# HGRN2 stage on one Trainium2 core: where ScalarE makes the high part of a head's second dense unit

## What is computed

```python
def hgrn2_mixer(h, w_in, lb, gn_g, w_out):
    z = h @ w_in
    q, f_raw, i, g = jnp.split(z, 4, axis=-1)
    f = lb + (1.0 - lb) * jax.nn.sigmoid(f_raw)
    log_f = jnp.log(f)
    k = 1.0 - f
    ...
    # per head and chunk; bt is the running sum of log_f
        decay = jnp.exp(jnp.where(tril[:, :, None], diff, -jnp.inf))
        scores = jnp.einsum('bhtk,bhsk,bhtsk->bhts', qt, kt, decay)
        o = (jnp.einsum('bhts,bhsv->bhtv', scores, vt)
             + jnp.einsum('bhtk,bhkv->bhtv', qt * jnp.exp(bt), S))
    ...
    o = o * lax.rsqrt(jnp.mean(o * o, axis=-1, keepdims=True) + EPS)
    o = o * gn_g.reshape(HG_HEADS, HG_DV)
    o = o.reshape(B, T, D_HG) * jax.nn.silu(g)
    return o @ w_out
```

## Time and profile before

| | |
|---|---|
| median of 3 runs | 1831.57 us (1830.7 to 1832.07) |
| the profiled execution | 1832.15 us, its span 1830.4 us |
| busy: TensorE, VectorE, ScalarE, GpSimd | 1784.8, 837.5, 647.2, 719.2 us |
| granted TensorE clock, mean | 0.994 of full speed |
| HGRN2 stage (eight heads) | about 1155 to 1422 us from the span's start |

### The profile page before, as it was taken

The page is one execution under the profiler, slowest core; times in us unless marked ns, Lnnn a source line. Parts: engine busy times, 40 slices in busy tenths (PEclk is TensorE's granted clock), DMA queues, the critical chain, the costliest instruction groups (busy, mean ns, idle before and its releaser), DMA issues.

```text
span 1830.4 us, 23909 instructions
## 1 busy us (share of the span) xinstructions
PE 1784.8 (98%) x8198; PEld 1444.1 (79%) x8198; DVE 837.5 (46%) x1472; ACT 647.2 (35%) x930; POOL 719.2 (39%) x315
## 2 busy tenths in 40 slices
PE   8999999999999999999999999999999999999998
PEld 7788778888888784788888888777777788888886
DVE  4644565333333698533242335456565432322425
ACT  5545343222222431532222224454544432222222
POOL 3222225444444375344444353332322344344441
PEclk9999999999999999999999999999999999999999
DMA  8331123322232131233223233221221233232221
GB/s 217 90 96 50 56 71 104 102 94 92 92 102 93 58 98 36 77 96 114 93 84 107 84 103 92 70 81 57 70 67 46 78 113 97 80 115 92 91 93 46
DMA packets 149749, 160.00 MB, mean 87 GB/s; under 512 B 10147, under 2 KB 110999, under 8 KB 149695
## 3 DMA queue, kind: packets, MB, share of 16 engines
q1 hardware_dynamic: 148879, 158.50, 28.2%
q10 hardware_dynamic: 816, 0.79, 0.1%
HBM read 156.63 MB, written 2.62 MB: 87 GB/s over the span
## 4 chain that ended last, share of the span: by engine, by line
PE 52%; issue 30%; POOL 10%; DVE 6%; ACT 1%; POOLq 0%; DVEq 0%; ACTq 0%
PE ps L1095 46%; POOL wlo L585 9%; DVE ps L2000 2%; PE ps L1269 2%; PE ps L1403 2%; PE ps L1258 1%; DVE ss L1617 1%; DVE acc L1639 1%; DVE h_lo L1605 0%; PE ps L1233 0%; PE ps L1234 0%; POOL wlo L596 0%; DVE xT L1642 0%; DVE apad L1978 0%; DVE sq L1798 0%
## 5 line engine op out<-in xcount | busy, mean ns | idle before, releaser
L585 POOL TENSOR_TENSOR wlo<-raw,whi 128x1024 fp32r<-128x1024 f32 x272 | 654.8, 2422 | 1034.5 <-ACT whi L652 1020.3
L1095 PE MATMUL ps<-h_hi,wlo 128*128 128x512 f32 x1472 | 589.7, 401 | 6.4 <-POOL wlo L585 4.2
L1095 PE MATMUL ps<-h_hi,whi 128*128 128x512 f32 x1472 | 576.3, 391 | 0.0
L1095 PE MATMUL ps<-h_lo,whi 128*128 128x512 f32 x1472 | 575.6, 391 | 0.0
L652 ACT ACTIVATE whi<-raw 128x1024 fp32r<-128x1024 f32 x282 | 292.0, 1054 | 504.8 <-PE ps L1095 504.8
L1095 PEld LDWEIGHTS ps<-h_hi,wlo 128*128 128x128 f32 x1472 | 277.6, 189 | 66.7 <-POOL wlo L585 5.1
L1095 PEld LDWEIGHTS ps<-h_hi,whi 128*128 128x128 f32 x1472 | 277.2, 188 | 59.3
L1095 PEld LDWEIGHTS ps<-h_lo,whi 128*128 128x128 f32 x1472 | 277.6, 189 | 58.3 <-issue 3.1
L1095 PE MATMUL ps<-m_hi,wlo 128*128 128x512 f32 x800 | 320.6, 401 | 1.5 <-DVE m_lo L1818 1.4
L1095 PE MATMUL ps<-m_hi,whi 128*128 128x512 f32 x800 | 317.1, 396 | 0.0
L1095 PE MATMUL ps<-m_lo,whi 128*128 128x512 f32 x800 | 317.1, 396 | 0.0
(11 more groups left out here) (259 smaller groups left out, 1426.7 us busy)
## 6 DMA issues: line engine op xcount, KB each, us to landing
raw<-in_ffn_w SPq DMA_DIRECT2D x264, 256.0 KB, 2.9
raw<-in_w_ff SPq DMA_DIRECT2D x128, 256.0 KB, 2.9
raw<-in_hg_w_in SPq DMA_DIRECT2D x64, 256.0 KB, 3.2
raw<-in_w_in SPq DMA_DIRECT2D x40, 256.0 KB, 4.1
raw<-in_cp_w_in SPq DMA_DIRECT2D x24, 256.0 KB, 3.0
raw<-in_w_out SPq DMA_DIRECT2D x16, 256.0 KB, 2.9
raw<-in_cp_w_out SPq DMA_DIRECT2D x16, 256.0 KB, 3.0
raw<-in_hg_w_out SPq DMA_DIRECT2D x16, 256.0 KB, 2.9
```

Of the source, the lines that this page charges most:

```text
L585: pool.tensor_tensor(wlo[:, u % RING, :, :], raw[:, u % RING, :, :], whi[:, u % RING, :, :].bitcast(F32), ALU.subtract).then_inc(unit_lo, 1)
L1095: mm = pe.matmul(ps[:, b, :], wt[:, s, a, m * P:(m + 1) * P], xt[:, kts[a], :], start=starts and a == 0 and i == 0, stop=last)
```

## The change

In `core` on ScalarE, `units(1)` moves from behind `level_rows(0)` to the front, ahead of `head_norm` and `level_rows(0)`. In the last head's table of dense tiles on TensorE, one tile more is made behind level three (index 2: tiles 8 to 10 in place of 8 and 9), one less behind level six (index 5: tile 15 alone in place of 14 and 15); those between keep their number and move on by one.

```diff
+                units(1)
                 if before_it is not None:
                     head_norm(before_it)
                 level_rows(0)
-                units(1)
                 act.wait_ge(filled[5], nth("hg", "vt", n))
...
             core(HG_HEADS - 1, lambda lo, hi: pieces_of(lo, hi, hgout), HG_HEADS - 2,
-                 ((4, 6), (6, 8), (8, 10), (10, 12), (12, 14), (14, 16), (16, 17), (17, 18), (18, 20), (20, 24)))
+                 ((4, 6), (6, 8), (8, 11), (11, 13), (13, 15), (15, 16), (16, 17), (17, 18), (18, 20), (20, 24)))
```

## The result

The changed kernel takes **1818.2 us** in the median of four runs (1817.56 to 1823.12), the kernel before 1831.82 (four runs, 1830.7 to 1832.66): a ratio of 0.9932 with a 95% interval of 0.9914 to 0.995, about 13.6 us less. The forecast was 1818.4, with a range of 1815.8 to 1821.9. The median lies within it; one of the four runs, 1823.12 us, lies outside.

What follows compares the result with a forecast made beforehand. TensorE, busy 98% of 1830.4 us, was taken as the bound, with its waits for rows to win. Six steady heads at 1.9 plus 1.85 for the last gave 13.2 us off 1831.57: 1818.4 us, range 1815.8 to 1821.9.

Steps and rivals of the forecast that it cites:

- The bound and the cause: HGRN stage: TensorE waits for ScalarE's rows (15.7 us) because GpSimd's subtraction holds the first-level key product 1.85 us.
- (c): Rival: the 1.85 us belong to the first level's fine stride, the copy only changes place; 1831.6 us, chance 0.03.
- The cover of the copy: ScalarE, steady head: moved copy costs zero, with 0.9 us left before the norm and 0.7 us more behind level-one rows.
- Where the collision goes: Steady head: GpSimd waits and ends at 1265.3, or the spans' doubling waits and ends near 1265.0; neither costs anything.
- The margin before the key product: VectorE, steady head: 0.9 us left between the moved collision and the key product at 1266.24.
- A steady head: Six steady heads: each wins 1.9 us, as level two starts earlier on TensorE.
- the bound 1.85 of my own two: Steady head: gain if the VectorE and ScalarE chain holds all the way, 1.85 us instead of 1.9.
- The last head: Chain-bound, gains 1.85 us; the moved tile, bounded by 0.62 won and 0.70 lost, is taken as 0.
- The first head: Level one 0.7 to 0.9 us late, absorbed by TensorE's 2.83 us wait; clock gain between 0 and 1.3, taken as 0.
- its staying up: Rival: first head's TensorE clock stays up, 1.3 us more, 14.5 us in all or 1817.1 us; chance 0.13.
- The sum: Whole kernel: 6 x 1.9 + 1.85 = 13.25, rounded to 13.2 us; span 1817.2, median 1818.4 us.
- (d): Rival: in-order ScalarE stands at the moved wait, released late; at 1265.7 it is 7.0 us slower, 1838.6 us; chance 0.03.

Runs made afterwards that it cites:

- e3: Kernel before, ScalarE's order kept, with GpSimd's subtraction of the moved unit held until VectorE has grown all seven levels: 1814.72 us, ratio 0.9908.
- e4: Changed kernel, with GpSimd's subtraction of the moved unit held until ScalarE has copied the values (vh), about its old place: 1829.49 us, ratio 0.9983.
- e8: Changed kernel plus loads of another ScalarE table and back (2.56 us) between moved copy and norm, heads two to eight: 1824.73 us, ratio 0.9958.
- e2: Kernel before with the second hunk alone (last head's tile moved, copy at its old place): 1832.18 us, ratio 1.0001.
- e1: Changed kernel without its second hunk (copy moved, last head's tiles as before): 1818.35 us, ratio 0.9917.
- e7: Changed kernel with the same ScalarE table load written twice between moved copy and norm, heads two to eight; only one took place: 1817.14 us.
- e6: Changed kernel with one more ScalarE table load (1.28 us) between moved copy and norm, heads two to eight: 1822.77 us in its one execution.
- v1: Changed kernel with both first-head copies made earlier, the first ahead of the gates, the second ahead of the table load: 1814.13 us, ratio 0.9901.
- v2: e3 with the first head's first copy made ahead of the gates: 1813.91 us, ratio 0.9899.

## Why the prediction was right, and where it was not

- **The bound and the cause** held: the key product was held by GpSimd's subtraction, 1.85 us a head. Holding the subtraction away from the product (e3) and back upon it (e4) shows it from both sides, and the rival that the first level is slow by itself (c) is out: 0.426 us.
- **The cover of the copy** held: copy forecast at 1261.1 against a first dense matmul at 1260.64, measured 0.30 us of waiting behind the table's load, so 0.3 us after its end; 0.9 us of idle time left, measured 0.93. The total cover was put at 1.6 us and e8 says 1.4 to 1.5.
- **Where the collision goes** was given with two ends, and the second came: the doubling waits (2.61 us), and GpSimd is held by the query besides (2.62 instead of 2.38). The margin before the key product was put at 0.9 us and is 1.12. One reading was wrong: the trace of before does hold a subtraction that finds VectorE in such a product. The second one of the first head starts at 1166.50 us, 0.34 before the end of the key product, and takes 2.54 us, the first 2.40; the earlier trace rows show them as one line. So the rows of before already held what came after: GpSimd held up by a VectorE product. The two subtractions, shortest, median and longest in ns:

```profile
L585 POOL TENSOR_TENSOR wlo<-raw,whi x2: 2397/2470/2544, 1164.2 to 1166.5; 128x1024 fp32r<-128x1024 f32 x2
```

- **A steady head**: 1.9 us forecast; measured 1.82 in the head that was followed and 1.84 in the mean of six (11.04 us against 11.4, 0.4 too much). The mis-sized term is the 0.05 us by which I let TensorE and not the chain set level two. Level two of the changed kernel starts at 1262.52, after its operand, and still has the longer form of a product that waited (0.72 us, not 0.62), so the bound 1.85 of my own two was the nearer one; the gain at level two is 3.75 - 1.90 = 1.85.
- **The last head**: 1.85 forecast, 1.84 measured, and the tile at zero, with the wait before level seven where it was foretold (0.50 us; I had 0.7).
- **The first head** was the step that failed in the profiled execution. I took 0 for the clock and gave its staying up 13 in 100; it stayed up, 1.5 us. Level one was 0.6 us late (I had 0.7 to 0.9), and the idle time was not the same in all: 0.46 + 2.11 = 2.57 us, before 2.83. But no argument by the length of the gaps alone would do: the clock falls in some executions and not in others with the same two gaps (below). It was a toss-up that I treated as a constant.
- **The sum** for the profiled execution: 11.04 + 1.84 + 1.5 = 14.4, against 13.2. It began the stage 0.25 us later than the kernel before, so 14.1 us are won at the end of the last head and 14.3 in the span. The median's 13.6 lies nearer to the forecast than this, and that is luck as far as these runs can tell: the runs of the changed kernel spread by 5.6 us, so a median of four does not settle half a microsecond.
- **The slower side** (d), by a late release, did not come. e8 shows the price of a late norm and late `rows` beyond the cover, and e4 that of a late subtraction; a late copy itself was not run.

## What to carry to other kernels

When one instruction of a group with the same shape is long, look at what the neighbour engine runs and compare the ends: here a VectorE product that was held ended 0.28 us after GpSimd's subtraction, wherever that lay. What counts is then when the neighbour's instruction runs: move the step that feeds it, or hold it back as in e3, so that the collision falls where VectorE waits anyway, and check that place for the same kind of operation. Before moving anything, measure the cover on the queue that it moves along; and a chain that passes through a wait makes moving filler work worth nothing.

## What the runs showed of the hardware

- GpSimd's subtraction and a VectorE product of two SBUF operands hold each other up. VectorE second: it ends 0.28 to 0.29 us after GpSimd in every such pair of the stage, in every run, and 0.42 us became 2.61. GpSimd second: 2.38 became 2.62 us where it began 0.37 us before the end of the decayed query, and 2.40 became 2.54 where it began 0.34 us before the end of a key product. VectorE instructions with one operand in PSUM are not held: in the kernel before, a drain (line 2144) at 1255.22 takes 0.69 us under subtractions that run from 1252.28 to 1259.39, and one at 1158.99, with none running, takes 0.69 too; so do all 14 drains of the stage that lie under a subtraction and the 18 that lie clear of one. This agrees with the Trainium skill ("SBUF — State Buffer", "Who interferes with whom"), by which the engine that issued first has the shared pair for its whole instruction. Only with GpSimd second do the rows fall short of that: it was held for 0.24 of the 0.37 us and 0.14 of the 0.34 us that VectorE's instruction still took.
- The granted clock of the first head is a matter of the execution. With one idle gap of 2.83 us before level two it fell in two profiles of two (the kernel before, 0.54; e2, 4.12 us from level two to level three). With gaps of 0.46 and 2.11 or 2.12 us it stayed up in five (the changed kernel, its repeat, e1, e4, e7: 2.64 or 2.65 us) and fell in two (e6, e8: 4.20 us, against 2.65), though the gaps before level two are the same there. In e3, v1 and v2, with less than 0.7 us idle before level two, it stayed up in all three. So the first head's collision costs its stall and, in some executions, 1.5 us of clock more; what decides between the two is not shown. TensorE of e6, levels two and three, and the stretch between them at half clock:

```profile
1172.86 0.82 PE L1503 MATMUL ps<-kq,rows 128*128 128x128 f32 x4 [2.11 <-ACT rows L1012]
1177.06 0.61 PE L1503 MATMUL ps<-kq,rows 128*128 128x128 f32 x4
...
1173.70:1176.50 2.80, 2.80 (x8) 2.13 (x8) 1.74 (x7) 0.62 (x2) 0.00 (x0) 0.50 0.66 186
```

- A second load of the table that ScalarE already has is not in the trace (e7), so it can't serve as padding; one of another table and one back take 1.28 us each, with the norm right behind them (e8).
- Executions of one kernel differ by up to 6 us (1829.54 to 1835.68 for the kernel before). In e6's, 4.9 us of span longer than the changed kernel's, 1.5 us are that clock; 2.9 us arose before the stage, where level one of the first head starts at 1168.63 instead of 1165.75. Of these, 1.8 us are there by the last `csig` instruction of ScalarE (line 880, at 693.76 instead of 692.00), and 1.1 arise from there to the first `pdiff` (line 894, at 714.20 instead of 711.32), where the granted clock over 690 to 712 us is 0.84 instead of 0.92. In e8 these two start at 694.22 and 714.66, and the clock is 0.84 as well. The first 1.8 us, and the last 0.4 behind the stage, are not explained.
